# Start-up of a streaming encoder step: later chunks of x issued behind the first one's landing, first weights split ahead of x's blocks, each quarter of the first tile behind its own chunk

## The reference: what is computed

```python
def rms_norm(x, g):
    xf = x.astype(jnp.float32)
    y = xf * lax.rsqrt(jnp.mean(xf * xf, axis=-1, keepdims=True) + EPS)
    return (y * g.astype(jnp.float32)).astype(x.dtype)
...
aq, ak, av, mq, mk, mv, mi, mf, mo = split_in(xn @ w_in)
...
x = x + mix @ w_out
u = jax.nn.relu(rms_norm(x, norm2_g) @ w_up)
return x + jnp.square(u) @ w_down
```

## Time and profile before

| what | value |
| --- | --- |
| time, median of 3 runs | 1756.48 us (1756.47 to 1756.99) |
| span of the profiled execution | 1756.4 us |
| PE busy | 1748.8 us (100%) |
| DVE, ACT, POOL busy | 893.6, 674.3, 179.1 us |
| the chain that ended last, by engine | PE 99% |
| granted TensorE clock, mean | 1.000 |

### The profile page before, as it was taken

The page is one execution under the profiler, slowest core; times in us unless marked ns, Lnnn a source line. Parts: engine busy times, 40 slices in busy tenths (PEclk is TensorE's granted clock), DMA queues, the critical chain, the costliest instruction groups (busy, mean ns, idle before and its releaser), DMA issues.

```text
span 1756.4 us, 27186 instructions
## 1 busy us (share of the span) xinstructions
PE 1748.8 (100%) x9302; PEld 1586.7 (90%) x9302; DVE 893.6 (51%) x1710; ACT 674.3 (38%) x1272; POOL 179.1 (10%) x237
## 2 busy tenths in 40 slices
PE   9999999999999999999999999999999999999999
PEld 7999998889997789999888999888999888999887
DVE  5634776666677646454344454344444334545333
ACT  5323754444354444333333333333333333333332
POOL 3301010001121210110000110000111000111000
PEclk9999999999999999999999999999999999999999
DMA  7675469998788553444334443334443334444442
GB/s 181 190 182 147 123 161 227 202 198 220 197 255 256 149 145 112 129 119 131 120 131 120 125 125 122 129 124 127 120 128 122 130 121 129 122 122 129 139 149 96
DMA packets 380177, 261.54 MB, mean 149 GB/s; under 512 B 91676, under 2 KB 327388, under 8 KB 380108
## 3 DMA queue, kind: packets, MB, share of 16 engines
q1 hardware_dynamic: 353190, 222.09, 44.3%
q0 software_dynamic: 11856, 34.68, 7.3%
q10 hardware_dynamic: 15062, 3.86, 1.1%
HBM read 244.90 MB, written 21.46 MB: 152 GB/s over the span
## 4 chain that ended last, share of the span: by engine, by line
PE 99%; DMA 0%; DVE 0%; issue 0%; ACTq 0%; ACT 0%; DVEq 0%
PE acc L521 18%; PE acc L522 18%; PE acc L523 18%; PE bank L608 8%; PE bank L609 8%; PE bank L607 8%; PE bank L1885 3%; PE ssb L607 2%; PE ssb L608 2%; PE ssb L609 2%; PE ssb L1885 1%; PE bank L567 1%; PE bank L568 1%; PE bank L566 1%; PE acc L566 1%; PE acc L568 1%
## 5 line engine op out<-in xcount | busy, mean ns | idle before, releaser
L501 DVE TENSOR_TENSOR w_lo<-raw,w_hi 128x512 fp32r<-128x512 f32 x768 | 556.5, 732 | 785.4 <-ACT w_hi L492 784.8
L492 ACT ACTIVATE w_hi<-raw 128x512 fp32r<-128x512 f32 x768 | 482.7, 630 | 834.6 <-PE acc L523 406.7
L522 PE MATMUL acc<-x2g_lo,w_hi 128*128 128x384 f32 x1024 | 348.0, 340 | 0.0
L521 PE MATMUL acc<-x2g_hi,w_hi 128*128 128x384 f32 x1024 | 345.8, 338 | 0.0
L523 PE MATMUL acc<-x2g_hi,w_lo 128*128 128x384 f32 x1024 | 344.6, 337 | 0.0
L521 PE MATMUL acc<-a_hi,w_hi 128*128 128x400 f32 (+1 forms) x768 | 268.1, 349 | 0.2 <-DVE w_lo L501 0.2
L522 PE MATMUL acc<-a_lo,w_hi 128*128 128x400 f32 (+1 forms) x768 | 262.9, 342 | 0.0
L523 PE MATMUL acc<-a_hi,w_lo 128*128 128x400 f32 (+1 forms) x768 | 262.3, 342 | 0.0
L608 PE MATMUL bank<-w_lo,a_hi 128*128 128x512 f32 x640 | 253.0, 395 | 0.0
L609 PE MATMUL bank<-w_hi,a_lo 128*128 128x512 f32 x640 | 252.6, 395 | 0.0
L607 PE MATMUL bank<-w_hi,a_hi 128*128 128x512 f32 x640 | 252.0, 394 | 0.0
(11 more groups left out here) (339 smaller groups left out, 1498.0 us busy)
## 6 DMA issues: line engine op xcount, KB each, us to landing
raw<-in_w_up SPq DMA_DIRECT2D x128, 512.0 KB, 4.0
raw<-in_w_down SPq DMA_DIRECT2D x128, 512.0 KB, 3.6
raw<-in_w_in SPq DMA_DIRECT2D x94, 512.0 KB, 4.6
raw<-in_w_out SPq DMA_DIRECT2D x32, 512.0 KB, 4.1
vc<-in_cache_v POOLq DMA_DIRECT2D x32, 256.0 KB, 7.3
kc<-in_cache_k SPq DMA_DIRECT2D x128, 64.0 KB, 3.3
state_blocks<-in_state_C POOLq DMA_DIRECT2D x16, 256.0 KB, 4.4
C_blk<-state_blocks SPq DMA_DIRECT2D x4, 1024.0 KB, 8.8
```

Of the source, the lines that this page charges most:

```text
L492: e.activation(w_hi[:, q], raw[:, slot, 4 * (q % 2):4 * (q % 2) + 4, :], ACT.Copy).then_inc(hi_ready, 1)
L501: e.tensor_tensor(w_lo[:, q], raw[:, slot, 4 * (q % 2):4 * (q % 2) + 4, :], w_hi[:, q].bitcast(F32), ALU.subtract).then_inc(lo_ready, 1)
L521: e.matmul(out, w_hi[:, q, kk], hi[:, k, at], start=k == 0, stop=False, skip_group_check=True)
L522: e.matmul(out, w_hi[:, q, kk], lo[:, k, at], start=False, stop=False, skip_group_check=True)
```

## The change

SP now also issues the prompt rows of chunk 2 that ACT issued before, and ACT no longer issues x_sample of chunk 2. ACT issues its rows of chunk 0, waits until these have landed (`x_rows0`, a semaphore of its own), and then issues its rows of chunk 1. Its rows of chunk 3 are issued behind the blocks of chunk 0. On ACT and DVE the weights of quarter q now come ahead of the blocks of chunk q. On PE `keep_busy(4)` is `keep_busy(3)`, `keep_busy(2)` is gone, and quarter q is multiplied between the turns of chunk q and those of chunk q + 1; each k waits for its own bank instead of four banks at once. POOL waits for chunk 3's two semaphores.

```diff
-X_TURNED = (range(8, 12), range(12, 16), (), ())
-X_AHEAD, X_LATER = range(0, 4), (range(4, 8), range(8, 12), range(12, 16), ())
-X_PIECES = (6, 3, 3, 3)
+X_CHUNKS = (range(0, 4), range(4, 8), range(8, 12), range(12, 16))
+X_PIECES, X_ROWS = (3, 1, 3, 1), (3, 2, 0, 2)
...
             e.wait_ge(S("x_in3"), 16 * X_PIECES[3])
+            e.wait_ge(S("x_rows3"), 16 * X_ROWS[3])
...
-                if c != 2:
-                    e.dma_start(xn[:, 0, cs], xs[:, cs]).then_inc(there, 16)
+                if c == 2:
+                    e.dma_start(xn[:, 2, cs], xp[P - META:2 * P - META, cs]).then_inc(there, 16)
+                    e.dma_start(xn[META:P, 1, cs], xp[0:P - META, cs]).then_inc(there, 16)
+                e.dma_start(xn[:, 0, cs], xs[:, cs]).then_inc(there, 16)
...
-            for c in range(4):
-                cs = slice(4 * c * P, 4 * (c + 1) * P)
-                e.dma_start(xn[:, 2, cs], x_prompt[0, P - META:2 * P - META, cs]).then_inc(S(f"x_in{c}"), 16)
-                at = 0 if c else X_HALF
-                e.dma_start(xn[META + at:P, 1, cs], x_prompt[0, at:P - META, cs]).then_inc(S(f"x_in{c}"), 16)
-                if c == 2:
-                    e.dma_start(xn[:, 0, cs], x_sample.rearrange("b t d -> (b t) d")[:, cs]).then_inc(S("x_in2"), 16)
+
+            def load_x_rows(c):
+
+                cs, at = slice(4 * c * P, 4 * (c + 1) * P), 0 if c else X_HALF
+                e.dma_start(xn[:, 2, cs], x_prompt[0, P - META:2 * P - META, cs]).then_inc(S(f"x_rows{c}"), 16)
+                e.dma_start(xn[META + at:P, 1, cs], x_prompt[0, at:P - META, cs]).then_inc(S(f"x_rows{c}"), 16)
                 if c == 0:
                     e.wait_ge(S("tail_zero"), 1)
-                    e.dma_start(xn[0:TAIL, 3, cs], x_prompt[0, 2 * P - META:SEQ, cs]).then_inc(S("x_in0"), 16)
-            read_out(e, "g1")
+                    e.dma_start(xn[0:TAIL, 3, cs], x_prompt[0, 2 * P - META:SEQ, cs]).then_inc(S("x_rows0"), 16)
+
+            load_x_rows(0)
+            e.wait_ge(S("x_rows0"), 16 * X_ROWS[0])
+            load_x_rows(1)
...
-            x_hi(X_AHEAD)
-            split_hi(e, 0, 0, after=lambda q: x_hi(X_LATER[q]))
+            def first_tile(q):
+
+                if q == 0:
+                    read_out(e, "g1")
+                x_hi(X_CHUNKS[q])
+                if q == 0:
+                    load_x_rows(3)
+
+            split_hi(e, 0, 0, after=first_tile)
...
-            x_lo(X_AHEAD)
-            split_lo(e, 0, 0, after=lambda q: x_lo(X_LATER[q]))
+            split_lo(e, 0, 0, after=lambda q: x_lo(X_CHUNKS[q]))
...
-            keep_busy(4)
+            keep_busy(3)
             e.wait_ge(S("g1_in"), 16)
             turn("g1", [(0, g1_rows[:])])
-            turn_x(range(0, 4))
-            keep_busy(2)
-            e.wait_ge(S("x_small"), 32)
-            turn_x(range(4, 8))
-            x_there = lambda q: read_out(e, *[("xT", 4 * q + x) for x in range(4)])
-            mm_tile(e, 0, 0, a_hi, a_lo, at=LIVE, before=x_there, after=lambda q: turn_x(X_TURNED[q]))
+            turn_x(X_CHUNKS[0])
+
+            def next_chunk(q):
+
+                if q == 0:
+                    e.wait_ge(S("x_small"), 32)
+                if q < 3:
+                    turn_x(X_CHUNKS[q + 1])
+
+            mm_tile(e, 0, 0, a_hi, a_lo, at=LIVE, each=lambda k: read_out(e, ("xT", k)), after=next_chunk)
```

More of the change, by code:

```diff
@@ L1902, in turn_x @@
                     e.wait_ge(S(f"x_in{k // 4}"), 16 * X_PIECES[k // 4])
+                    if X_ROWS[k // 4]:
+                        e.wait_ge(S(f"x_rows{k // 4}"), 16 * X_ROWS[k // 4])
                     b = fill(e, ("xT", k))
```

## The result

| | changed kernel | kernel before, same chip |
| --- | --- | --- |
| median | 1761.64 us (8 runs, 1760.64 to 1762.92) | 1756.52 us (8 runs, 1756.24 to 1758.33) |
| ratio | 1.0029, 95% interval 1.0020 to 1.0038 | |

The change costs 5.1 us, 0.29%. The forecast was 1756.3 us with a range to 1758.9, so the time lies 2.7 us beyond the range, on the slower side.

What follows compares the result with a forecast made beforehand. PE was taken as the bound, with 7.6 us idle in all. The gain 13.77 - t1, with t1 = max(13.4, 13.6) = 13.6, was 0.17 us: 1756.48 - 0.17 = 1756.3 us, range 1754.8 to 1758.9.

Steps and rivals of the forecast that it cites:

- The frame: On PE, which runs through from 30 us on, the change is worth what it moves the start of that run.
- 13.4: Start-up on PE: quarter 0 done at 9.25 + 1.35 + 2.26 + 0.53 = 13.4 us.
- 4.17: Start-up on PE: a chunk takes 3.59 + 0.05 + 0.53 = 4.17 us, where it was 3.9.
- Tile 1's stall behind ACT's squares: In tile 1 PE waits 1.3 us for the last `w_lo`: saved filler returns as a stall behind ACT.
- chunk 3's rows and the small parameters: Both issued later in the start-up at no cost; chunk 3's rows have until 21.9, 9.9 us.
- the base: Profile of the kernel before: span 1756.4 us, chunk 1's transposes on PE at 13.26 after 1.22 us idle.
- t1: Start of chunk 1's transposes on PE: 13.26 us before, forecast 13.6 after the change.
- its own formula: Gain at tile 1's last quarter on PE: 33.88 - 20.11 - t1 = 13.77 - t1, forecast 0.17 us.
- Then chunk 1's landing: ACT's 480 KB of chunk 1, issued at 8.35, land at 13.6, estimated between 12.2 and 18.7.
- ACT's issue is held by SP's: Rival near 8.3 us: SP's long issue delays ACT's by up to 3.5 us; t1 17.1, time 1759.8; chance 0.03.
- the clock rival: Rival: TensorE's clock falls in the start-up for lack of products; 1758.1 us, or 1762.1 if long; chance 0.14.
- late-chunk rival: Rival: chunk 1 lands 9.9 us after issue, t1 18.7, time 1761.4; chance 0.04, within 0.10 for late landings.

Runs made afterwards that it cites:

- swapped: The changed kernel with SP issuing chunk 1's prompt rows and ACT issuing chunk 2's behind chunk 0's landing: 1758.24 us, ratio 1.0009.
- the filler run: The changed kernel with two filler products added behind chunk 0's transposes: 1761.54 us, ratio 1.0028.
- the DMAs alone: DMAs issued as in the changed kernel, but PE, ACT and DVE in the order of before with both fillers: 1763.05 us, ratio 1.0038.
- no wait: The changed kernel without ACT's wait for chunk 0's landing before it issues chunk 1's rows: 1757.81 us, ratio 1.0008.
- order only: DMAs issued as in the kernel before, with the changed order on PE, ACT and DVE and the changed filler: 1759.06 us, ratio 1.0013.
- the two in the order of before: DMAs of swapped, with PE, ACT and DVE in the old order and both fillers: 1756.53 us; the same with one filler product for two between chunks: 1756.65 us.
- the changed kernel again: The changed kernel, unchanged, run once more for a second profile: 1762.1 us (one run).

## Why the prediction was wrong

**What held.** The frame did: only the start-up counts, and it can be read off one point. The span minus the start of chunk 3's turns is 1734.4 to 1734.6 in the seven executions with the changed order, and 1735.3 to 1735.5 in the five with the old one, that of the earlier trace rows among them (1756.4 - 21.07 = 1735.3). So the order gives back 0.9 us behind chunk 3; the prediction's own terms say 33.88 - 21.07 less 20.11 - 8.34, 1.04. PE was done with quarter 0 at 14.1 (15.77 - 1.68), 13.5 without the wait and 13.4 with the chunks swapped, where "13.4" stood; most of the 0.7 us by which it was late in the changed kernel is that `w_hi` began at 9.63 and not 9.25. A chunk takes 4.28 to 4.35 us, not 4.17. Tile 1's stall behind ACT's squares is 36.25 - 26.51, the start of chunk 3's products, less four quarters of 2.1: 1.3 us, as forecast. That chunk 3's rows and the small parameters cost nothing held too.

**The first step that failed** is the base, the profiled execution that "agrees with the median of the timed runs to 0.1 us". That set a span beside a time. The usual t1 of before is 11.39 and not 13.26, and there was 1.9 us less to gain: by its own formula the prediction would have been 11.9 - t1, a loss of 1.7 us at t1 = 13.6, a time of 1758.2. The 1.22 us of idle ahead of chunk 1, on which the change seemed to have something to win, isn't there as a rule.

**The second** is "Then chunk 1's landing": 13.6, with SP's queue "taking half". It took all of it, for 4 us and more, and t1 came to 15.77, 2.2 us later. Either step alone gives a time inside the range, 1758.2 with the base put right and 1758.5 with t1 at 15.77; the two together do not. The rival "ACT's issue is held by SP's" had the right engines and was dismissed on the wrong evidence: a short issue in the earlier trace rows shows that ACT isn't kept waiting, and says nothing of when the first packet moves. The rate of q10 in the earlier trace rows did not help either, since its DMAs there were issued one beside the other with SP's and not behind them. The Trainium skill, Perfetto Trace Analysis, section DMA Instruction - HWDGE, warns that a DMA instruction that looks fast may still be waiting for the data movement; the changed kernel's 0.36 us of issue and more than 4 us to the first packet agree. The Trainium skill, DMA: Bandwidth & Descriptors, section Queues, rings and completion order, says that each DMA engine takes turns, packet by packet, between the queues that have work. From 13 to 16 us the trace agrees (436 packets of each queue). From 9 to 12 us it has none of q10: either the turns weren't taken, or ACT's DMAs had not yet become work for the engines, and no view here tells which.

**The sum.** 1.87 us of base (13.26 - 11.39), 2.17 of landing (15.77 - 13.6) and 0.37 from t1 to tile 1's last quarter (20.48 - 20.11) are 4.4, and 1756.3 + 4.4 = 1760.7 beside the 1760.64 of the profiled execution. The median is 1.0 us above that, and the profiles show two ways to it: the clock behind the wait for chunk 1 (1.15 us in the second profile) and a later landing of chunk 0 (1.0 us in the filler run's). Five of the eight executions show a mean clock of 0.999; how many of them lost time by it isn't shown. So the clock rival was real, but it needed a long wait more than it needed the missing filler: 0.999 or less stands in all five executions of the DMAs alone, which have all the filler, in 4 of 30 of the three kernels that lack filler and have chunk 1 in time (no wait, order only, swapped), and in none of 21 where chunk 1 is in time and the first filler is back (the two in the order of before).

The clock rival also rested on a misread row. "Before the longest such stretch was 2.1 us" leaves out the stretch from the end of the second filler, 12.03 (10.15 + 1.88), to the first product behind chunk 1's turns, 2.9 us; the clock stayed up over it.

**Where the 5.1 us come from.** Swapping the chunks takes away 3.4 (late rows and the clock behind them). Going back to the old order and filler from there takes away 1.7 (the fastest of ten executions swapped, 1757.99, is slower than the slowest of ten in the old order, 1757.15). In the two profiles it is the serial chain `w_hi`, `w_lo`, `x_lo`, product that now ends ahead of chunk 1's turns (t1 13.42 against 11.88) and 0.4 us more for each of two chunks, less the 0.9 given back. Nothing measurable is left. The late-chunk rival gave 1761.4 at t1 = 18.7, near the time measured, by two errors that cancel: the base 1.9 too late and t1 2.9 too late.

## What to carry to other kernels

Before a DMA is issued later on one engine, count the bytes that other engines have issued by then: here it began to move only behind most of them, and a short issue in the profile says nothing on that. Let the engine that issues without a wait carry the piece that is wanted first, and hold back one that is wanted later (3.4 us here), or hold both engines (2.6 us here). And set a profiled execution's time, not its span, against the median before taking its waits as the usual ones: a stall of one execution is no stall to be saved.

## What the runs showed of the hardware

A DMA issued by ACT moved its first packet more than 4 us behind its issue when SP had issued 2.7 MB ahead, 1.8 MB of it not yet moved, and 1.6 us behind it when SP had been held; in the meantime q1 had all of the engines' time. Once both queues moved, from 13 to 16 us, they moved packet for packet (436 and 436). TensorE's clock fell to its lower level behind a wait of 2.02 us (the filler run), of 2.77 us (the changed kernel again) and of 4.83 us (DMAs only); it stayed up behind those of 1.91 and 1.68 us in the changed kernel's first profile.
